# Other starting places within 64 bytes for the operands of the split matmuls

## The reference, cut to what matters

```python
# first_block, per layer l
h = x @ w_in[l]                       # 1024 -> 6048 columns, and 4096 for the gates
branches = rwkv7(...), mla(...), conv(...), memory_attention(...)
x = layer_norm(ALPHA * x + (sum(gates * (branches @ w_o_branch[l])) @ w_out[l]))
# second_block, per layer
x, xc = ffn_sublayer(x), ffn_sublayer(xc)        # swiglu: 1024 -> 2 x 2816 -> 1024
o = concat([neighbourhood, windowed, fourier]) @ w_out
x = x + gate * rms_norm(o)                        # xc too, except in the last layer
x, xc = ffn_sublayer(x), ffn_sublayer(xc)        # last layer: x alone
```

## The kernel before, in words

| operand | before | after |
|---|---|---|
| ring, hT, hidT (both models) | 32 | 32 |
| first model: xT / xT_low | 32 / 0 | 0 / 0 |
| first model: ws, slot 0 high / low | 0 / 0 | 32 / 32 |
| slot 1 high / low | 0 / 0 | 48 / 48 |
| slot 2 high / low | 0 / 0 | 16 / 40 |
| first model: brT / ext, work | 32 / 0 | 0 / 32 |
| second model: aT / aT_low | 32 / 32 | 32 / 0 |
| second model: ws, slot 0 high / low | 32 / 32 | 32 / 48 |
| slot 1 high / low | 32 / 32 | 0 / 16 |
| hs, places 0 and 2 high / low | 32 / 32 | 0 / 16 |
| hs, places 1 and 3 high / low | 32 / 32 | 32 / 48 |

## Time and profile before

### The profile page before, as it was taken

How to read it: one execution, slowest core, us unless ns; L and a number is a source line. 1 busy time by engine, 2 the same in 40 slices (tenths; PEclk the granted TensorE clock), 3 DMA queues, 4 the chain that set the end, 5 groups by cost and what they waited for, 6 DMA issues and landing times.

```text
span 2856.7 us, 43600 instructions
## 1 busy us (share of the span) xinstructions
PE 2735.9 (96%) x17521; PEld 2280.3 (80%) x17521; DVE 1010.4 (35%) x1586; ACT 653.5 (23%) x1218; POOL 1342.7 (47%) x608
## 2 busy tenths in 40 slices
PE   9999999999999997999999999999999999898998
PEld 7988777699777775888888778888888888775996
DVE  1752753246437333001350632002330023524237
ACT  3432212144321112000131542001130001425001
POOL 4830100067010003566646555566646566667786
PEclk9999999999999998999999999999999999999999
DMA  6556643455665444222223123223222322232453
GB/s 235 184 197 243 245 154 134 182 178 182 229 246 199 164 163 134 103 89 102 92 85 104 44 67 104 100 91 103 88 96 96 103 88 103 98 109 74 147 172 137
DMA packets 68612, 390.14 MB, mean 137 GB/s; under 512 B 19232, under 2 KB 20864, under 8 KB 22528
## 3 DMA queue, kind: packets, MB, share of 16 engines
q1 hardware_dynamic: 66640, 379.03, 37.3%
q10 hardware_dynamic: 1840, 9.18, 0.9%
HBM read 387.09 MB, written 1.10 MB: 136 GB/s over the span
## 4 chain that ended last, share of the span: by engine, by line
issue 25%; POOL 11%; POOLq 10%; PE 9%; DMA 3%; SPq 1%; DVE 1%; ACT 0%; DVEq 0%; ACTq 0%
POOL m_ws L1747 9%; POOLq L1746 7%; DMA m_ring<-in_panels 3%; PE m_bank L1913 2%; SPq L1703 1%; POOLq L1759 1%; PE m_bank L1830 1%; POOL m_ws L1765 1%; PE m_bank L1831 1%; PE m_bank L1832 1%; POOLq L1764 1%; POOLq L1771 1%; PE m_bank L2009 1%; PE m_bank L2010 1%; PE m_bank L2011 1%
## 5 line engine op out<-in xcount | busy, mean ns | idle before, releaser
L1830 PE MATMUL m_bank<-m_aT,m_ws 128*128 128x512 f32 (+1 forms) x1792 | 631.9, 353 | 35.2 <-DVE m_aT_low L2408 15.8
L1831 PE MATMUL m_bank<-m_aT_low,m_ws 128*128 128x512 f32 (+1 forms) x1792 | 628.6, 351 | 0.0
L1832 PE MATMUL m_bank<-m_aT,m_ws 128*128 128x512 f32 (+1 forms) x1792 | 628.3, 351 | 0.0
L1747 POOL TENSOR_TENSOR m_ws<-m_ring,m_ws 128x2048 fp32r<-128x2048 f32 x127 | 593.5, 4673 | 18.7
L1913 PE MATMUL m_bank<-m_ws,m_hs 128*128 128x512 f32 x1848 | 422.5, 390 | 3.5 <-DVE m_ws L2445 1.4
L1830 PEld LDWEIGHTS m_bank<-m_aT,m_ws 128*128 128x128 f32 x1792 | 345.6, 193 | 83.2 <-issue 23.8
L1913 PEld LDWEIGHTS m_bank<-m_ws,m_hs 128*128 128x128 f32 x1848 | 346.0, 188 | 79.4 <-issue 6.9
L383 POOL TENSOR_TENSOR m_ws<-m_ring,m_ws 128x2048 fp32r<-128x2048 f32 x48 | 221.3, 4625 | 342.2 <-ACT m_ws L910 341.9
L1832 PEld LDWEIGHTS m_bank<-m_aT,m_ws 128*128 128x128 f32 x1792 | 345.6, 193 | 42.6
L1831 PEld LDWEIGHTS m_bank<-m_aT_low,m_ws 128*128 128x128 f32 x1792 | 345.7, 193 | 41.8
L2451 DVE TENSOR_TENSOR m_hidT<-m_sg,m_bank 128x512 f32 (+3 forms) x88 | 54.7, 621 | 688.9 <-ACT m_sg L2218 688.9
(11 more groups left out here) (349 smaller groups left out, 3396.7 us busy)
## 6 DMA issues: line engine op xcount, KB each, us to landing
m_ring<-in_panels SPq DMA_DIRECT2D x350, 1024.0 KB, 4.8
m_rows<-m_gg_dram ACTq DMA_DIRECT2D x6, 1024.0 KB, 5.1
m_bias<-in_rpb SPq DMA_DIRECT2D x48, 64.0 KB, 2.6
m_ring<-in_panels SPq DMA_DIRECT2D x4, 512.0 KB, 4.5
m_hT<-in_ln_rows ACTq DMA_DIRECT2D x2, 1024.0 KB, 6.4
m_con<-in_con SPq DMA_DIRECT2D x1, 1536.0 KB, 10.5
memT_ctx<-in_memT SPq DMA_DIRECT2D x2, 512.0 KB, 4.9
x_tok<-in_x SPq DMA_DIRECT2D x1, 1024.0 KB, 13.1
```

What stands on the lines that cost most here:

```text
L1747: nc.gpsimd.tensor_tensor(ws[:, p, 1, :], ring[:, p, :], ws[:, p, 0, :].bitcast(F32), ALU.subtract)\
L1830: mm(out, w, a, start=start, stop=False)
L1831: mm(out, w, a_low, start=False, stop=False)
L1832: return mm(out, w_low, a, start=False, stop=stop)
```

## The change

It moves the starting places in the table above, and nothing else: no instruction is added, taken away or reordered. Padding tensors that nobody reads (`in_front_of_xT`, `in_front_of_work`, `in_front_of_aT_low`) push what follows. `in_front_of_work` has 64 elements, so that `work` still ends behind the longer `ws`. `hs` and the second `ws` get 4 and 20 more elements per part, the first `ws` becomes one row with a small table of gaps.

```diff
+        sb("in_front_of_xT", [P, 8])
         xT = sb("xT", [P, KD, T], F32R)
...
         with ExitStack() as place:
+            place.enter_context(nc.sbuf_tensor("m1_in_front_of_work", [P, 64], F32))
             work = place.enter_context(nc.sbuf_tensor("m1_work", [P, 73 * T], F32))
...
-        ws = sb("ws", [P, 3, 2, PAN], F32R)
+        ws_all = sb("ws", [P, 6 * PAN + 56], F32R)
         xT_low = sb("xT_low", [P, KD, T], F32R)
         sb("work_rest", [P, 17 * T])
+
+        def ws(slot_, part):
+            at = (2 * slot_ + part) * PAN + (0, 0, 4, 4, 12, 18)[2 * slot_ + part]
+            return ws_all[:, at:at + PAN]
...
-                    w = ws[:, c_ % 3, :, :].rearrange("p h (u k c) -> p h u k c", u=2, k=KD)
+                    w, w_low = (ws(c_ % 3, h).rearrange("p (u k c) -> p u k c", u=2, k=KD) for h in range(2))
...
-        ws = sb("ws", [P, 2, 2, PAN], F32R)
+        ws_all = sb("ws", [P, 2, 2, PAN + 20], F32R)
+        ws = ws_all[:, :, :, 0:PAN]
...
+        sb("in_front_of_aT_low", [P, 8])
         aT_low = sb("aT_low", [P, KD, T2], F32R)
...
-        hs = sb("hs", [P, HS, 2, T2], F32R)
+        hs_all = sb("hs", [P, HS, 2, T2 + 4], F32R)
+        hs = hs_all[:, :, :, 0:T2]
```

More of the change, by code:

```diff
@@ L382, in _ @@
                     pool.wait_ge(s["high_in"], l * SPLITS + c_ + 1)
-                    nc.gpsimd.tensor_tensor(ws[:, c_ % 3, 1, :], ring[:, PANEL[("in", c_)] % RING, :],
-                                            ws[:, c_ % 3, 0, :].bitcast(F32), ALU.subtract).then_inc(s["split_in"], 1)
+                    nc.gpsimd.tensor_tensor(ws(c_ % 3, 1), ring[:, PANEL[("in", c_)] % RING, :],
+                                            ws(c_ % 3, 0).bitcast(F32), ALU.subtract).then_inc(s["split_in"], 1)
                 pool.wait_ge(s["panel_used"], l * PANELS1 + PANEL[("in", 23)] + 1)
@@ L476, in split_panel @@
                             dst = out[:, u * T:(u + 1) * T]
-                            mm(dst, w[:, 0, u, k, :], xT[:, k, :], start=(k == 0), stop=False)
-                            mm(dst, w[:, 0, u, k, :], xT_low[:, k, :], start=False, stop=False)
-                            last = mm(dst, w[:, 1, u, k, :], xT[:, k, :], start=False, stop=(k == KD - 1))
+                            mm(dst, w[:, u, k, :], xT[:, k, :], start=(k == 0), stop=False)
+                            mm(dst, w[:, u, k, :], xT_low[:, k, :], start=False, stop=False)
+                            last = mm(dst, w_low[:, u, k, :], xT[:, k, :], start=False, stop=(k == KD - 1))
                     return last
@@ L909, in high @@
                     act.wait_ge(slot[n % RING], (l * (PANELS1 // RING) + n // RING + 1) * 16)
-                    a_(ws[:, c_ % 3, 0, :], ring[:, n % RING, :], ACT.Copy).then_inc(s["high_in"], 1)
+                    a_(ws(c_ % 3, 0), ring[:, n % RING, :], ACT.Copy).then_inc(s["high_in"], 1)
                 for n in range(2):
```

## The result

The changed kernel takes 2882.8 us (2 runs, 2882.05 to 2883.55) against 2854.77: a ratio of 1.0098, 95% interval 1.0069 to 1.0127. It is 1.0% slower, an interval clear of 1 but half of the 2% that the prediction called a difference. I had forecast 2832.2, 0.8% faster, in a range from 2774 to 2862.

A forecast was written before the change was run, and what follows sets the result against it. TensorE was taken as the bound. Savings of 9.9, 7.2, 1.2 and 4.3 us sum to 22.6 off the profiled 2856.7, giving 2834.1; less 1.9 for the runs' median, 2832.2 us, range 2774 to 2862.

The forecast's parts named there:

- What bounds the kernel, and that split passes lose 13.35 ns of a fixed kind: TensorE sets the pace; each fp32r matmul (three products per operand pair) loses 13.35 ns whatever its length.
- Is it tied to the place?: All split matmuls: the loss varies by 6.6 ns with where operands begin, and also with how two reads fall into step.
- the price of 6.6 ns: Split matmuls: a moving operand beginning at 0 of 64 bytes saves 6.6 ns against one at 32.
- That all operands of the second model begin at 32: Second model before the change: every operand begins at byte 32 of 64, where the remainder is largest.
- -7.2 and -4.3 us: Second model: 7.2 us saved at 512 columns with weights standing (aT_low to 0), 4.3 us with weights moving.
- First model: First model's 256-column split passes: xT moves from 32 to 0, two of three passes gain, 9.9 us saved.
- The price of the starts not seen: Starts at 16, 48 and 40, absent from the trace: between -11.05 and +6.6 ns a pass, taken as 0.
- GpSimd and the other engines unchanged: Moved parts written by GpSimd, VectorE and ScalarE: 1.1 us either way in the last layer, taken as zero.
- The last inner layer counted at nothing: 2645 to 2780 us, 256 columns: 1056 passes wait for GpSimd, so no gain was counted.
- (1): Split passes everywhere: weight load and moving read collide at equal places, nearly all loss goes, 75.5 us, 2779 us; chance 0.28.
- (2): Whole kernel: the loss is a cost of switching operands, nothing changes, 2855 us; chance 0.22.
- (3): Split passes with starts at 16, 48 or 40 touch one more piece: 28.1 us slower, 2883 us; chance 0.13.

The follow-up runs named there:

- aT_low_32_alone: Kernel before the change with only the second model's aT_low moved from 32 to 0 of 64 bytes, hs kept in place: 2877.1 us, ratio 1.0070.
- places_alone: Separate kernel without both models: 64 stretches of matmuls on TensorE alone, with chosen operand starts; 226.7 ns at equal places for 512 columns, total time without meaning.
- first_model_only: Kernel before the change with only the first model's moves (xT, ws, work), second model as before: 2859.3 against 2856.1 us, ratio 1.0011.

## Why the prediction was wrong, by its steps

- *What bounds the kernel, and that split passes lose 13.35 ns of a fixed kind*: held. The pace at 512 columns is TensorE's own, and the 25 us appear in it one for one.
- *"Is it tied to the place?"* Yes, but this step failed, the price of 6.6 ns for a moving operand at 0 of 64 bytes against one at 32. I took the triple of the earlier trace rows, the short step after L478, for the effect of a moving operand at 0 modulo 64, and made it a price of 6.6 ns. (Even the size is off by the rows themselves: 360 - 352.8 is 7.2, which would have made the sum 24.7 us instead of 22.6.) Modulo 256, which is what counts, that triple's places are xT 32, xT_low 128, ws 128; it is one of several patterns that settle at 256 columns, and says nothing for 512., the same addresses with another order of steps, was the warning: I wrote it down and kept the price. In `aT_low_32_alone` this very move, a moving operand from 32 to 0, took the triple from 226.7 to 231.0 ns a pass instead of bringing it down, and in `places_alone` equal places take 226.7 ns at 0 as at 32.
- *That all operands of the second model begin at 32*: I read this as the worst case. Modulo 256 their places before were ws 32 in all parts, aT 32, aT_low 32, hs 32, all equal, which is the best case at 512 columns. After: ws 32, 112, 192, 16; aT 96; aT_low 128; hs 128 to 240. Terms -7.2 and -4.3 us became +17.6 and +9.4.
- *First model* -9.9 us: +3.0 by the trace. Its places were no equal ones before either. One execution is weak ground for this term, since the same unmoved first model showed 118.0 ns a pass in one trace and 118.9 in another, 2 us over its 2256 passes; the 3.2 us of `first_model_only` bear it out.
- *The price of the starts not seen*: bounded at +6.6 ns, taken at 0 "by the nearest start". The bound was near what came (5.4 and 4.8 ns a pass in the changed kernel), by luck, since it was made of the misread triple; the value was not. With no row of the trace for any of them, and 4256 passes at stake, the upper bound alone was worth 28 us.
- *GpSimd and the other engines unchanged*: held, within 0.5%.
- *The last inner layer counted at nothing*: wrong by 2.5 us here.
- *Rivals*: (1) falls, no place gives the loss back at 512 columns. Its floor, (1.95 - 0.28)/15, is 111.3 and not 111.7 ns, which changes its sum by 1 us. (2) falls. Beside it I had put the Trainium skill, TensorE: Matmul & The Clock Gate, Step-by-step: what each phase is for, by which loading the next weights takes nothing from the running matmul's reading. I had drawn from it that no place of the weights matters, and that does not hold for these operands: with the moving operand fixed, moving the standing one by 16 bytes costs 6.7 ns. The prediction also says that the trace disagrees with the Trainium skill's N/2.4 + 2.5 ns (same page, Back-to-back issue gap) for split passes only; the plain fp32 ones, 429.3 ns for 512 columns, fit it only if each column counts twice. (3) had the sign and, at 2883, the number, with 0.13. Its mechanism is wrong: 32 and 64 bytes cost what 16 does. That its sum met the measurement is luck: 4256 passes at 6.6 ns, 28.1 us, where the kernel shows 5232 at about 5.2, 27.0.

What makes the step is open: why 512 columns want equal places and 256 don't, which pair of reads has to agree, and what the last 13.35 ns are. The experiments exclude the number of standing columns as its measure, and a place modulo 64.

## What to carry to other kernels

Before operands are moved, work out where they begin modulo 256 bytes, not modulo 64, and look at the pace from start to start: 226.7 ns at 512 columns is the least that any place gave here, and there every padding of one operand that was no multiple of 256 bytes cost the whole family 1.5 to 3%. At 512 columns give all float32r operands of a loop one place modulo 256; at 256 columns try differences of 64 bytes, and measure in the kernel itself, since the stretches alone did not foretell it. Padding put in for one tensor moves all that follow, so close it up to 256 bytes.

## What the runs showed of the hardware that I had not expected

- The pace of a float32r matmul depends on where moving and standing operand begin relative to each other, with a period of 256 bytes: 226.7 ns at equal places and 228.3 to 234.3 at the others for 512 columns, 113.3 to 123.5 at 256. It isn't the difference alone: the same one took 229.9 and 233.3 ns.
- The same addresses settle at different paces from one stretch to the next: 231.0 and 233.3 ns, or 352.8 and 340.1 ns a triple.
- Fewer standing columns made a matmul of 512 moving columns slower, 231.7 ns with 32 against 226.7 with 128.
